# Routing's second search on 50 pairs, and VectorE adding the halves of units 2 to 49 of an expert up-projection

## The reference, cut to what matters

```
q  = (h @ w_q).reshape(B, S, 8, 2, 128)
sc = einsum('bshpd,phnd->bshpn', q, keys)
v1, i1 = top_k(sc[..., 0, :], 16);  v2, i2 = top_k(sc[..., 1, :], 16)
cand = v1[..., :, None] + v2[..., None, :]          # 16 x 16 per token and head
cidx = i1[..., :, None] * 128 + i2[..., None, :]
best, pos = top_k(cand.reshape(..., 256), 16)
idx = take_along_axis(cidx, pos);  gates = softmax(best)
out = sum_k gates * gelu(h . u[idx]) * v[idx]       # 16384 experts
```

## Time and profile before

| | |
|---|---|
| runs | 1370.46, 1370.01, 1370.46 us |
| the profiled execution | 1370.27 us, of which the span of the trace is 1368.2 us |
| PE busy | 1346.7 us, 98% |
| DVE busy | 1046.5 us, 76% |
| ACT busy | 772.5 us, 56% |
| POOL busy | 291.4 us, 21% |
| granted clock | 0.999 of full speed |

### The profile page before, as it was taken

The page is one execution under the profiler, slowest core; times in us unless marked ns, Lnnn a source line. Parts: engine busy times, 40 slices in busy tenths (PEclk is TensorE's granted clock), DMA queues, the critical chain, the costliest instruction groups (busy, mean ns, idle before and its releaser), DMA issues.

```text
span 1368.2 us, 25383 instructions
## 1 busy us (share of the span) xinstructions
PE 1346.7 (98%) x10066; PEld 1264.4 (92%) x10067; DVE 1046.5 (76%) x1848; ACT 772.5 (56%) x1271; POOL 291.4 (21%) x176
## 2 busy tenths in 40 slices
PE   9999999999999999999999999999999999999997
PEld 7989989999989999999999999999998798899986
DVE  5556575595998999999999888887887764777754
ACT  5674645556575555554444456555677654655543
POOL 6000000298973222220000033320132000100001
PEclk9999999999999999999999999999999999999999
DMA  7443366466669877775555689987443543555562
GB/s 249 140 137 124 126 199 215 140 201 200 197 215 326 292 248 246 254 258 183 187 186 186 190 320 356 349 306 246 142 155 108 184 145 119 174 187 188 189 191 105
DMA packets 76581, 279.17 MB, mean 204 GB/s; under 512 B 8496, under 2 KB 8752, under 8 KB 76208
## 3 DMA queue, kind: packets, MB, share of 16 engines
q1 hardware_dynamic: 67104, 243.73, 53.7%
q0 software_dynamic: 9216, 33.56, 6.6%
q10 hardware_dynamic: 144, 0.26, 0.0%
HBM read 276.47 MB, written 1.05 MB: 203 GB/s over the span
## 4 chain that ended last, share of the span: by engine, by line
PE 83%; DVE 9%; ACT 4%; issue 1%; POOL 1%; DMA 0%; SPq 0%; POOLq 0%; DVEq 0%; ACTq 0%
PE bank L495 82%; ACT A L1275 2%; DVE wlo L1912 2%; DVE A L1912 1%; ACT whi L1275 1%; PE bank L504 1%; ACT L1275 1%; DVE A L2181 1%; DVE A L2195 1%; DVE A L2196 1%; DVE A L2188 0%; DVE A L2174 0%; DMA raw<-in_w_in_t 0%; DVE bank L1912 0%; POOL wlo L2865 0%
## 5 line engine op out<-in xcount | busy, mean ns | idle before, releaser
L495 PE MATMUL bank<-hT,whi 128*128 128x256 f32 (+2 forms) x4140 | 993.3, 322 | 5.9 <-POOL wlo L2865 3.0
L495 PE MATMUL bank<-hT,wlo 128*128 128x224 f32 (+1 forms) x2952 | 796.7, 270 | 0.0
L495 PEld LDWEIGHTS bank<-hT,whi 128*128 128x128 f32 x4140 | 693.3, 188 | 35.5 <-POOL wlo L2865 4.3
L1912 DVE TENSOR_TENSOR wlo<-raw,whi 128x1024 fp32r<-128x1024 f32 (+1 forms) x386 | 472.0, 1224 | 215.2 <-ACT whi L1275 212.4
L1275 ACT ACTIVATE whi<-raw 128x1024 fp32r<-128x1024 f32 (+1 forms) x450 | 472.5, 1052 | 258.3 <-PE bank L495 245.5
L495 PEld LDWEIGHTS bank<-hT,wlo 128*128 128x128 f32 x2952 | 560.7, 190 | 0.0
L2865 POOL TENSOR_TENSOR wlo<-raw,whi 128x1024 fp32r<-128x1024 f32 x62 | 148.5, 2400 | 111.1 <-ACT whi L1275 108.4
L1275 ACT ACTIVATE A<-bank 128x224 f32<-128x224 f32 (+3 forms) x233 | 99.7, 433 | 120.4 <-PE bank L495 110.8
L1275 ACT ACTIVATE first_cut<-bank 128x224 fp32r<-128x224 f32 x126 | 45.0, 357 | 144.2 <-PE bank L495 140.9
L2881 POOL DMA_INDIRECT A<-in_v,small x32 | 51.6, 1613 | 286.1 <-DVE A L1908 174.0
L2881 POOL DMA_INDIRECT A<-in_utab,small x32 | 52.6, 1643 | 132.1 <-DVE A L1915 130.6
(11 more groups left out here) (187 smaller groups left out, 1436.0 us busy)
## 6 DMA issues: line engine op xcount, KB each, us to landing
raw<-in_u SPq DMA_DIRECT2D x128, 512.0 KB
raw<-in_v SPq DMA_DIRECT2D x128, 512.0 KB
raw<-in_w_up SPq DMA_DIRECT2D x44, 512.0 KB
raw<-in_w_down SPq DMA_DIRECT2D x22, 512.0 KB
raw<-in_w_in_t SPq DMA_DIRECT2D x17, 512.0 KB
raw<-in_w_in_g SPq DMA_DIRECT2D x16, 512.0 KB
raw<-in_w_out SPq DMA_DIRECT2D x16, 512.0 KB
raw<-in_w_pq SPq DMA_DIRECT2D x16, 512.0 KB
```

Of the source, the lines that this page charges most:

```text
L495: return e.matmul(o, l, r, start=st, stop=sp_, skip_group_check=True)
L1912: return e.tensor_tensor(o, a, b, op)
```

## The change

1. **Second search on 50 pairs.** Of the 16 x 16 sums, only those can be among the 16 largest for which (i+1)(j+1) is at most 16: 50 pairs. Seven additions build blocks of them (`BEST_BLOCKS`), and the search runs over rows of 50. A position is turned into row and column by comparing it with the rows' first positions: comparing with "at least" and multiplying by steps of the payload (`pay`, from differences of the first index and 256 times the row's length) gives, in one sum, the first index and the offset of the row, which two operations with a large constant part again. The second index is found as before. The constants (`first16`, `steps16`, `iota16` times 256) come by one more transfer of 16 KB, into a tile `tabs` in the place of a gap.
2. **26 steps a block** in place of 30, on all engines: the second search has steps 12 to 14; the two index lookups have three steps each (15 to 20), each half of 1024 elements; the division is step 21; PE transposes in step 23; ScalarE's exponential is in step 18; the reading and casting of the transposes has three steps (24 to 26). Routing thus ends in unit 48.
3. **VectorE adds the halves in units 2 to 49** (`ADDED`). PE has no identity product for them. ScalarE copies the low half into one of two buffers in `og` (and waits for the addition of two units ago, which frees the buffer), VectorE adds it to the second half into `acts`, in its iteration n+1 ahead of its step of routing, and this frees the bank (`u_sum`). ScalarE applies Gelu in place in `acts`.
4. **Gathers** are issued in unit 51 at the earliest; before, the first was in unit 50.

```diff
+ADDED = range(2, 50)
-    GATHERS.setdefault(_u - 5, []).append(_g)
+    GATHERS.setdefault(max(_u - 5, REP_AT), []).append(_g)
+BEST_OF = [16 // (i + 1) for i in range(16)]
+NBEST = sum(BEST_OF)
+BEST_BLOCKS = [(0, 1, 16), (1, 1, 8), (2, 1, 5), (3, 1, 4), (4, 1, 3), (5, 3, 2), (8, 8, 1)]
         def u_freed(n):
+            if n in ADDED:
+                return u_summed(n)
...
 PE, wide:
-                        if k == JOIN_AT and u:
+                        if k == JOIN_AT and u and u - 1 not in ADDED:
                             join(u - 1)
...
 ScalarE:
             def take_low(n):
+                if n in ADDED:
+                    if n - 2 in ADDED:
+                        e.wait_ge(*u_summed(n - 2))
+                    e.wait_ge(s["w"], BASE["u"] + n + 1)
+                    act(u_part2(n), banks[4 + n % 3][:, 0:TD], ACT.Copy).then_inc(s["u_low"], 1)
+                    return
...
             def take_high(n, func):
...
+                elif func == ACT.Gelu:
+                    take_sum(n)
+            def take_sum(n):
+                e.wait_ge(*u_summed(n))
+                act(acts[:, n, :], acts[:, n, :], ACT.Gelu).then_inc(s["ev_act" if n % 2 else "u_even"], 1)
...
 VectorE, routing:
+                own(ts(step, iv[:, :, 0, :], -1.0, None, ALU.mult))
+                for i, n, w in BEST_BLOCKS:
+                    shape = [P, 8, n, w]
+                    own(tt(c50[:, :, at:at + n * w].rearrange("p h (n w) -> p h n w", n=n),
+                           vv[:, :, 0, i:i + n].unsqueeze(3).to_broadcast(shape),
+                           v2p[:, :, 0:w].unsqueeze(2).to_broadcast(shape), ALU.add))
+                own(tt(step[:, :, 1:16], step[:, :, 1:16], iv[:, :, 0, 0:15], ALU.add))
+                own(tt(pay, step, tabs[:, 16:32].unsqueeze(1).to_broadcast([P, 8, 16]), ALU.add))
...
-                yield from top16(t3(cand, 8), t3(candw, 8), bv, pu, 8, 4)
+                yield from top16(c50, w50, bv, pu, 8, 8, True)
+                own(ts(p256, posu[:, 0:P].bitcast(U32), 256.0, None, ALU.mult))
...
+                    compare(0)
+                    times(0)
+                    yield
+                    total(0)
+                    compare(1)
+                    yield
+                    times(1)
+                    total(1)
+                    if q == 0:
+                        own(ts(split, both16, -TO_256, None, ALU.add))
+                        own(stt(sel_i[0], split, TO_256, both16, ALU.add, ALU.subtract))
+                        own(stt(posf[:, 0:P], split, TO_256, p256, ALU.add, ALU.add))
                     yield
...
 VectorE, in the loop over units, ahead of its step of routing:
+            def add_low(u):
+                n = u - 1
+                if n in ADDED:
+                    e.wait_ge(s["u_low"], n + 1)
+                    tt(acts[:, n, :], banks[4 + n % 3][:, TD:2 * TD], u_part2(n), ALU.add).then_inc(s["u_sum"], 1)
+                pick_u(u)
```

More of the change, by code:

```diff
@@ L231, in build @@
         wlo = [sb(f"wlo{i}", UNIT, F32R) for i in range(NSPL)]
-        keep = sb("keep", NKEEP)
+        keep = sb("keep", NREST)
         sb("gap2", 24)
@@ L400, in build, with u_part2, joined, u_summed @@
         u_part = first_cut[:, 3 * T:3 * T + TD]
+        def u_part2(n):
+            return og[:, 2 * TD * (n % 2):2 * TD * (n % 2 + 1)].bitcast(F32)
+        def joined(n):
+            return sum(i not in ADDED for i in range(n))
+        def u_summed(n):
+            return (s["u_sum"], n - ADDED[0] + 1)
         def u_freed(n):
+            if n in ADDED:
+                return u_summed(n)
             return (s["ev_act"], PAIR_FREED[PAIR["u"] + n // 2][1]) if n % 2 else (s["u_even"], n // 2 + 1)
@@ L851, in routing @@
             def routing(b):
-                for _ in range(29):
+                for _ in range(22):
                     yield
@@ L859, in routing @@
                 free[b] = (s["rt_dve"], 4 * b + 3)
-                yield
+                for _ in range(4):
+                    yield
             def gates(half):
@@ L1446, in routing @@
             def routing(b):
-                for _ in range(21):
+                for _ in range(17):
                     yield
@@ L1756, in act_program @@
                     hi(BASE["u"] + u + 2)
[L1757 to L1758 removed]
+                    take_sum(late)
                 late = u - 2 if "exp" in side.marks else None
@@ L2169, in hgrn, with top16 @@
                 yield
-            def top16(src, work, vals, idxs, n, per):
+            def top16(src, work, vals, idxs, n, per, joined=False):
                 again()
@@ L2176, in top16 @@
                         own(ins)
-                    if j % per == per - 1:
+                    if j % per == per - 1 and not joined:
                         yield
@@ L2198, in top16 @@
                         own(ins)
-                    if j % (per // 2) == per // 2 - 1:
+                    if j % (per // 2) == per // 2 - 1 and not (joined and j == n - 1):
                         yield
@@ L2228, in routing @@
                 yield
+                both16 = scw[:, 400:400 + P]
                 for q in range(2):
[L2230 to L2239, removed]
-                    yield
-                    again()
-                    own(e.tensor_reduce(t3(sel_i[q], 8), t4(oh2, 8, 16), AX, ALU.add))
+                    ps = t3(posf[:, 0:P] if q else p256, 8)
+                    ref = (banks[7][:, 144:160], banks[7][:, 0:16])[q].unsqueeze(1).unsqueeze(1)
@@ new lines, in routing, with compare @@
+                    worth = iv[:, :, 1, :] if q else pay
+                    found = sel_i[1] if q else both16
+                    def compare(h):
+                        again()
+                        for g in (2 * h, 2 * h + 1):
+                            own(tt(t4(banks[g][:, :], 2, 16),
+                                   ps[:, 2 * g:2 * g + 2, :].unsqueeze(3).to_broadcast([P, 2, 16, 16]),
+                                   ref.to_broadcast([P, 2, 16, 16]), ALU.is_equal if q else ALU.is_ge))
@@ new lines, in times, with total @@
+                    def times(h):
+                        again()
+                        for g in (2 * h, 2 * h + 1):
+                            own(tt(t4(oh2[:, g * 512:(g + 1) * 512], 2, 16), t4(banks[g][:, :], 2, 16),
+                                   worth[:, 2 * g:2 * g + 2, :].unsqueeze(2).to_broadcast([P, 2, 16, 16]), ALU.mult))
+                    def total(h):
+                        again()
+                        own(e.tensor_reduce(t3(found[:, 64 * h:64 * h + 64], 4),
+                                            t4(oh2[:, 1024 * h:1024 * h + 1024], 4, 16), AX, ALU.add))
```

56 lines of the change are left out of this document (34 added, 22 removed).

## The result

The changed kernel takes 1372.52 us, the median of 22 runs (fastest 1371.54), against 1370.49 for the kernel before (22 runs): a ratio of 1.0013, 95% interval 1.0007 to 1.0019. It is 2.0 us slower, where 7.0 were forecast. One of its 22 runs took 3763.89 us, in a slow state; the ratio leaves it out, and the median of the other 21 is 1372.39. The profiled execution took 1371.64 us with a span of 1369.6, so it shows 1.4 us of the difference; it is one of the fastest of its 22, and where the rest arises in the others no trace shows.

A forecast was written before the change was run, and what follows sets the result against it. PE and DVE were taken as two full engines side by side, PE newly waiting for DVE. Terms: -5.3 - 2.6 - 1.24 (today's Exp stalls) + 7.1 (block 0) + 9.3 (block 1) = +7.3, giving 1377.5 us, range 1365.5 to 1381.

The forecast's parts named there:

- Identity products: Up-projection on PE: 48 products of 0.11 us removed from PE's path, a gain of 5.3 us.
- Stalls after unit 51 gone: PE stalls after 400.51 and 407.71 us should go, from later gathers and an earlier search end: 2.6 us gained.
- the surge: DVE's steps 11 to 20, units 10 to 18: 29.2 us with nine additions against 22.6, so 6.6 us behind.
- the slack: How late DVE's addition may be before PE stands still waiting for the bank: 3.95 us.
- Bank waits: PE waiting for DVE's addition to free a bank: 2.3 us in block 0, 4.5 in block 1 with inherited lag.
- Exp: After ScalarE's exponential, table load waits for unit 16's addition: stall of 2.7 us in place of 0.62, in both blocks.
- Steps 24 to 26 in block 1: Narrow casts and scalings on DVE held up by GpSimd: 2.1 us of PE stall, as in block 0.
- port wait: DVE operation held until GpSimd's operation ends; one forecast in step 24, three in step 25.
- The clock: Granted clock is 1.00 in every stretch that matters, so clock effects were left out.
- casts: DVE's narrow casts and scalings in steps 24 to 26: 2.1 us of PE stall in each block.
- the second rival: Surge is there but port waits fall into gaps, no carried lag: 1371 us (1368.5 to 1373), chance 0.18.
- The first rival: DVE keeps up, steps 11 to 20 with additions taking at most 26.5 us: 1362.8 us (1361 to 1366), chance 0.18.

The follow-up runs named there:

- e5: Changed kernel with VectorE's additions in units 2 to 11 only, identity products in 12 to 49; 1368.66 us, ratio 0.9984 to the kernel before.
- e1: Changed kernel with only the additions undone, every unit having its identity product again; 1369.55 us, ratio 0.9991 to the kernel before.
- e4: Changed kernel with steps 24 and 25 cast straight from the bank and step 26's small operations through a bank; 1366.54 us, ratio 0.9972 to the kernel before.
- e6: Changed kernel with double steps after units 2 and 26 instead of 12, 26 and 40; 1369.15 us, ratio 0.9991 to the kernel before.
- e8: Kernel before, with its 256-wide search and 30 steps, plus additions in units 2 to 49 and later gathers; 1376.25 us, ratio 1.0041 to the kernel before.
- e7: Changed kernel with steps 24 to 26 through banks, double steps after units 2 and 26, high part ahead of Gelu; 1361.24 us, ratio 0.993 to kernel before.
- e2: Changed kernel with ScalarE making the weights' high part ahead of the waiting Gelu after Exp; 1374.38 us, ratio 1.0027 to the kernel before.
- e3: Changed kernel with steps 24 and 25 casting and scaling straight from the transposes' bank, one copy less; 1373.61 us, ratio 1.0021 to the kernel before.

## Why the prediction was wrong, point by point

- **Identity products**: forecast 48 x 0.11 = 5.3 us; measured 0.12 each, 5.8 (e5 shows it alone).
- **Stalls after unit 51 gone**: forecast 2.6, measured 2.57, and nothing is late next there. Right. In e1 another wait took their place. Two readings that the prediction gives to rows 5 stand elsewhere in the trace before; GpSimd's and DVE's timelines:

```profile
401.30 2.37 POOL L2865 TENSOR_TENSOR wlo<-raw,whi 128x1024 fp32r<-128x1024 f32 x1
...
405.02 1.21 DVE L1912 TENSOR_TENSOR wlo<-raw,whi 128x1024 fp32r<-128x1024 f32 x1
```

- **DVE's work in the surge, and the slack**: 28.6 us against 29.2, the second search 7.5 as forecast (290.51 to 298.34 less one addition), and PE begins to stand when the lag passes 4 us. Bank waits 1.72 against 2.3 in block 0 and 4.07 against 4.5 in block 1, with 2.5 of them inherited, as the sum had it (e4). The 0.6 us lie in steps 15 to 20: 15.7 where 16.3 were forecast. The prediction's own terms, 6.6 less 3.95, are 2.65; it puts 2.3 without a reason, and the same sum with 28.6 gives 2.05 where 1.72 was measured. Mechanism shown by e1, e4, e6 and e8; sizes within 0.6.
- **Exp, the step that failed most**: "In the changed order ScalarE there first waits for the addition of unit 16", and then the load, 2.7 us in each block. The load is not behind the wait: it was issued at 308.29, 2.4 us ahead of the addition's end, and hides in the wait. 1.34 us in each block (with the clock's part of unit 43 taken off, as e4 has it); 2.7 us of the error.
- **Steps 24 to 26 in block 1**: forecast 2.1 us; measured 0. One operation of four slipped into a gap, and the lag in unit 47 (3.49 us from ScalarE's copy to the addition) stayed under the slack. In block 0 2.15 against 2.1: right. 2.0 us of the error. This term hangs by a threshold: by an estimate from these rows, one more port wait of 2.3 us in block 1 (3.49 + 2.3 less 3.95) would have made its stall 1.8 us.
- **The clock was left out.** "Clock effects are left out" was true of the kernel before, and not of one with a stall of 3.74 us: 0.2 us here, 1.6 in e6.

Together: 7.3 less 0.5 (identity), 1.0 (banks), 2.7 (Exp) and 2.0 (casts), and 0.2 for the clock, is 1.3, the measured difference of the stages. The direction and, but for the casts of block 1, the places were right. The time lies by that of the second rival (1371), but not for its reason: the port waits are there, and it was the Exp term and the cover of block 1 that were too large. The first rival fell at its own point of decision, 26.5 us of work in the surge where 28.6 were measured; e7, which has no bank wait and no Exp stall either, lies 1.6 us under its 1362.8.

## What to carry to other kernels

When a full engine is made to wait for another, average load says little: work out the lag step by step against the slack, since the two double steps inside the surges went with 5.8 us of bank waits that moving them gave back (e6); 3.4 us of it are left in the time. A stall on one engine opens gaps in which others run freely; taking it away alone can cost more than it was worth (e2, e3), so remove the contention before the stall. For short VectorE operations beside a busy GpSimd, one operand in PSUM can be worth much: e4 has as many operations as the changed kernel and is 6 us faster.

## What was not expected of the hardware

- VectorE's casts, copies, scalings and SCALAR_TENSOR_TENSOR (STT) of 32 to 128 columns with all operands in SBUF took 0.16 to 0.3 us alone, and otherwise until GpSimd's running operation had ended, up to 2.5. Not every operation in SBUF is held up: eight MAX8 over 128 columns took 0.27 to 0.28 each in e4 (328.76 to 330.39), six of them inside GpSimd's operation of 329.12 to 331.52. No operation with an operand in a bank was held up in steps 24 to 26 of e4, among them STT with the second input in SBUF (0.29). The price is the rest of GpSimd's operation, up to 2.5 us for 0.2 of work. The Trainium skill (SBUF — State Buffer, "SBUF: two separate sides") speaks of an exclusive lock that one instruction holds to its end and the other fully waits for. The traces agree: each of the four long operations of block 0 ends within 0.15 us behind one of GpSimd's.
- A table load is not held back by the wait of the activation behind it (308.29 against 310.73). The load takes 1.28 us, and no pause stands around it: the copy ahead ends at 308.27, and behind the load of 304.72 the exponential starts at 306.02. The Trainium skill (ScalarE: Activation LUTs, "What ACT_TABLE_LOAD costs") gives the same load and a drain of about 1380 ns beside it; the drain is not in these traces.
- PE's clock fell to the 1.2 GHz level, with products 0.59 us apart instead of 0.31, for 3.4 us each time, after stalls of 3.74 (the changed kernel, e3) and 2.90 us (e2) and e8's waits of 3.1 and 3.0, and in e2 for 6.8 us from 379.1 on, 1.4 us before the end of its stall of 3.74. It stayed at 2.4 GHz after 1.55 us (e4), 2.09 (the changed kernel) and 2.29 (e3), yet fell after the first 2.09 in e6, and not after the second, ahead of unit 51. What tells these apart stays open.
